# Third block of a three-block decoder: the 16 meta rows stored in zero-padded tiles of 128 rows

## The reference, cut to what matters

```
x = first_block(x, ...)            # gated linear attention, sliding window, MoBA
x = second_block(x, ...)           # mixers, dense and expert feed-forward, gated inputs
return third_block(x, meta_tokens_3, ...)

third_block:
    h = concat([meta (16 rows), x (256 rows)])         # 272 keys
    h = h + hybrid_mixer(rmsnorm(h))    # 8 heads of latent attention (MLA) and
                                        # 8 heads of sparse attention (DSA: an index picks
                                        # 64 keys for each query)
    h = h + swiglu(rmsnorm(h))
    return rmsnorm(h)[:, 16:]
```

## Time and profile before

| | us |
|---|---|
| median of 3 runs | 1898.78 |
| lowest and highest run | 1895.74, 1899.84 |
| span of the profiled execution, first to last instruction | 1895.5 |
| TensorE busy | 1844.5 (97%) |
| DVE, ACT, POOL busy | 1401.9, 1203.6, 67.4 |

### The profile page before, as it was taken

The page is one execution under the profiler, slowest core; times in us unless marked ns, Lnnn a source line. Parts: engine busy times, 40 slices in busy tenths (PEclk is TensorE's granted clock), DMA queues, the critical chain, the costliest instruction groups (busy, mean ns, idle before and its releaser), DMA issues.

```text
span 1895.5 us, 31983 instructions
## 1 busy us (share of the span) xinstructions
PE 1844.5 (97%) x11013; PEld 1598.6 (84%) x11013; DVE 1401.9 (74%) x2038; ACT 1203.6 (64%) x1897; POOL 67.4 (4%) x106
## 2 busy tenths in 40 slices
PE   8999999999999999999999999999999999999998
PEld 7969889899989888888788888888887898789997
DVE  5575765865566768998989898989899677565555
ACT  6556555544456557877777787877777665354444
POOL 2000000000000020000000000000000034000000
PEclk9989999999999989999999999999999999999999
DMA  8526334465546459999999999999999342136552
GB/s 299 192 90 220 114 134 132 143 199 188 188 156 212 147 189 367 371 371 363 365 371 371 364 372 363 360 366 359 365 361 332 123 146 89 34 100 200 184 192 91
DMA packets 129571, 454.05 MB, mean 240 GB/s; under 512 B 15182, under 2 KB 20206, under 8 KB 129216
## 3 DMA queue, kind: packets, MB, share of 16 engines
q1 hardware_dynamic: 119920, 435.74, 65.1%
q10 hardware_dynamic: 8544, 13.30, 2.2%
q0 software_dynamic: 1008, 3.67, 0.5%
HBM read 450.53 MB, written 5.27 MB: 240 GB/s over the span
## 4 chain that ended last, share of the span: by engine, by line
PE 91%; DVE 5%; ACT 3%; issue 1%; DMA 0%; ACTq 0%; DVEq 0%
PE ps L276 27%; PE ps L277 27%; PE ps L278 27%; PE ps L1069 2%; PE ps L1052 1%; DVE low L261 1%; PE ps L2737 1%; DVE xT_low L342 1%; PE ps L973 1%; PE ps L2803 1%; PE ps L1080 1%; PE ps L410 1%; ACT xT_high L330 1%; ACT high L252 1%; PE ps L309 0%
## 5 line engine op out<-in xcount | busy, mean ns | idle before, releaser
L261 DVE TENSOR_TENSOR low<-ring,high 128x1024 fp32r<-128x1024 f32 x828 | 978.9, 1221 | 213.1 <-ACT high L252 210.9
L252 ACT CAST high<-ring 128x1024 fp32r<-128x1024 f32 x828 | 833.3, 1050 | 191.6 <-PE ps L278 161.4
L276 PE MATMUL ps<-high,xT_high 128*128 128x256 f32 (+2 forms) x1848 | 639.7, 346 | 19.2 <-DVE xT_low L342 6.5
L277 PE MATMUL ps<-low,xT_high 128*128 128x256 f32 (+2 forms) x1848 | 622.7, 337 | 0.0
L278 PE MATMUL ps<-high,xT_low 128*128 128x256 f32 (+2 forms) x1848 | 619.9, 335 | 0.0
L276 PEld LDWEIGHTS ps<-high,xT_high 128*128 128x128 f32 (+1 forms) x1848 | 347.3, 188 | 61.7 <-issue 14.2
L278 PEld LDWEIGHTS ps<-high,xT_low 128*128 128x128 f32 (+1 forms) x1848 | 347.4, 188 | 40.4
L277 PEld LDWEIGHTS ps<-low,xT_high 128*128 128x128 f32 (+1 forms) x1848 | 348.2, 188 | 33.2
L276 PE MATMUL ps<-high,smallT_high 128*128 128x512 f32 (+2 forms) x582 | 225.2, 387 | 0.8 <-DVE smallT_low L342 0.5
L277 PE MATMUL ps<-low,smallT_high 128*128 128x512 f32 (+2 forms) x582 | 225.2, 387 | 0.0
L278 PE MATMUL ps<-high,smallT_low 128*128 128x512 f32 (+2 forms) x582 | 224.3, 385 | 0.0
(11 more groups left out here) (353 smaller groups left out, 1435.0 us busy)
## 6 DMA issues: line engine op xcount, KB each, us to landing
ring<-in_stream SPq DMA_DIRECT2D x828, 512.0 KB, 5.1
bias_rows<-bias_line ACTq DMA_DIRECT2D x2, 1536.0 KB, 13.5
wide<-in_wide_rows ACTq DMA_DIRECT2D x5, 512.0 KB, 5.6
work<-bias_rows ACTq DMA_DIRECT2D x2, 1024.0 KB, 9.7
h<-in_x SPq DMA_DIRECT2D x2, 512.0 KB, 4.9
work<-bias_rows ACTq DMA_DIRECT2D x2, 512.0 KB, 6.5
token_rows<-mix ACTq DMA_DIRECT2D x1, 1024.0 KB, 4.6
consts<-in_consts ACTq DMA_DIRECT2D x1, 870.0 KB
```

Of the source, the lines that this page charges most:

```text
L252: A.e.copy(k.high[:, slot, cols], k.ring[:, slot, cols]).then_inc(flow.high_made, 1)
L261: V.e.tensor_tensor(k.low[:, slot, cols], k.ring[:, slot, cols], k.high[:, slot, cols].bitcast(F32), ALU.subtract).then_inc(flow.split, 1)
L276: T.e.matmul(out, x[0], w[0], start=start, stop=False, **more)
L277: T.e.matmul(out, x[0], w[1], start=False, stop=False, **more)
```

## The change

The meta rows get tiles of full height. `probM` has 128 rows instead of 16; POOL sets it, the meta area of `proj` and the third tile of `kv` to zero, after DVE has left the experts (`experts_left`); ACT waits for `meta_cleared` before its first evacuation in the third block. The transposes of the meta rows read 128 rows and write 128 columns, of which the next transpose overwrites the last 112. The products of the meta block contract over 128 rows.

```diff
-        self.probM = buf("probM", [META, 2, NT, P])
+        self.probM = buf("probM", [P, 2, NT, P])
...
 def key_columns(dst, src):
-    return ([(src(NT)[0:META], META)] + [(src(t), P) for t in range(NT)], dst)
+    return ([(src(NT), META)] + [(src(t), P) for t in range(NT)], dst)
...
-                ins = T.e.transpose(k.ps[0:width, self.banks[n % nb], at:at + rows], src,
-                                    k.const("ident", rows)[:, 0:rows])
+                ins = T.e.transpose(k.ps[0:width, self.banks[n % nb], at:at + P], src, k.const("ident"))
                 at += rows
...
-        ins = A.e.copy(k.probM[:, h % 2, :, :].rearrange("p b w -> p (b w)"), a.meta_rows(k))
+        ins = A.e.copy(k.probM[0:META, h % 2, :, :].rearrange("p b w -> p (b w)"), a.meta_rows(k))
...
 def after_experts_dve(V, k):
     moe_add_dve(V, k, 1 if V.again else 0)
+    V.tell(V.e.memset(k.small[0:1, 222:223], 0.0), k.s["experts_left"])
     turn_first_dve(V, k, "ple1")
...
+        self.meta_rows = k.proj[:, 5120:6368]
+        self.meta_values = self.meta_rows[:, 736:1248]
...
-            lambda h, b: self.kv[0:self.blocks[b][1], tile_of[b], h * P + 64:(h + 1) * P], self.blocks,
+            lambda h, b: self.kv[:, tile_of[b], h * P + 64:(h + 1) * P], self.blocks,
...
-                return self.prm[:, 736 + h * 64:736 + (h + 1) * 64]
+                return self.meta_values[:, h * 64:(h + 1) * 64]
...
 # block3_pe, the index keys (and likewise the rotary keys, 128:160, into bank 6)
-    for rows, src in ((META, b3.prm[:, 160:224]), (P, b3.pr[:, 0, 160:224]), (P, b3.pr[:, 1, 160:224])):
-        ins = T.e.transpose(k.ps[0:64, INDEX_JOB_BANKS[0], at:at + rows], src, k.const("ident", rows)[:, 0:rows])
+    for rows, src in ((META, b3.meta_rows[:, 160:224]), (P, b3.pr[:, 0, 160:224]), (P, b3.pr[:, 1, 160:224])):
+        ins = T.e.transpose(k.ps[0:64, INDEX_JOB_BANKS[0], at:at + P], src, k.const("ident"))
...
 # block3_act
     scaled(A, k)
+    A.e.wait_ge(*A.next(k.s["meta_cleared"]))
     evac3_act(A, k, b3, 0, 0, 224)
...
 # block3_pool
+    G.e.wait_ge(k.s["experts_left"], 1)
+    G.step(G.e.memset(b3.meta_rows, 0.0))
+    G.step(G.e.memset(b3.kv[:, NT, :], 0.0))
+    G.tell(G.e.memset(k.probM[:, :, :, :], 0.0), k.s["meta_cleared"])
     G.e.wait_ge(k.s["evac"], evac + 1)
```

More of the change, by code:

```diff
@@ L129 @@
     "added all_chosen angled angles_made bias_loaded bias_made centred chosen_made cleared conv_high conv_low "
-    "conv_made conv_z copied counted diagonal diff down_high down_loaded down_made down_ready down_split ends "
+    "conv_made conv_z copied counted diagonal diff experts_left down_high down_loaded down_made down_ready down_split ends "
     "evac expd exped exps ffn_added ffn_made final_done final_loaded gained gated gated_mm gla_done gla_made "
@@ L133 @@
     "ke_made kept ki_copied ki_turned kr_copied kr_turned kv_added left line_stored logged masked masked_l "
-    "meta_parts meta_turned mixed mla_roped normed ones_set out_stored outed p_loaded params parts_high parts_low "
+    "meta_parts meta_turned mixed meta_cleared mla_roped normed ones_set out_stored outed p_loaded params parts_high parts_low "
     "plain pool_roped probs_turned prod prod_out qk_roped reduced relu_made root route_made routed router_loaded "
@@ L3143, in keys_job @@
     def keys_job(self, dst, lo, mlo, width):
-        return [(self.prm[:, mlo:mlo + width], META)] + [(self.pr[:, t, lo:lo + width], P) for t in range(NT)], dst
+        return [(self.meta_rows[:, mlo:mlo + width], META)] + [(self.pr[:, t, lo:lo + width], P) for t in range(NT)], dst
     def mla(self, k):
@@ L3375, in after5 @@
             at = 0
-            for rows, src in ((META, b3.prm[:, 128:160]), (P, b3.pr[:, 0, 128:160]), (P, b3.pr[:, 1, 128:160])):
-                ins = T.e.transpose(k.ps[0:32, 6, at:at + rows], src, k.const("ident", rows)[:, 0:rows])
+            for rows, src in ((META, b3.meta_rows[:, 128:160]), (P, b3.pr[:, 0, 128:160]), (P, b3.pr[:, 1, 128:160])):
+                ins = T.e.transpose(k.ps[0:32, 6, at:at + P], src, k.const("ident"))
                 at += rows
```

## The result

| | before | after |
|---|---|---|
| median of 5 runs each | 1898.78 | 1883.54 |
| span of the profiled execution | 1895.5 | 1880.8 |

The ratio is 0.9925, 95% interval 0.9913 to 0.9937: 14 us faster (15.2 in the medians), where 9.4 were forecast, and outside the forecast range. Two more sets of five runs of the same changed kernel gave 0.9946 (0.9933 to 0.9958) and 0.9928 (0.9916 to 0.9941). The mean of the three is 0.9933, 12.7 us. That is the gain to be explained, 3.3 us more than forecast. One of the 85 later runs of the kernel before took 3625.42 us at full clock, for a reason that isn't known; it is in no figure here.

The account below looks back on a forecast made before the run. TensorE was taken as the bound. Savings of 4.3 + 3.5 + 1.1 + 0.2 + 0.5 less 0.2 for POOL made 9.4 us, so 1898.8 became 1889.4 us; range 1886 to 1893 (0.72), 8 in 10 from 1885 to 1896.

Parts of the forecast that it names:

- The price of a change of row count: On TensorE, each change of row count between neighbouring instructions was taken to cost some 0.14 us.
- MLA products: Ten products per MLA head, 8 heads: 0.55 us saved in seven and 0.46 in the first, 4.3 us.
- the plain 0.112: Time taken for each TensorE product of 128 rows that follows one of equal row count: 0.112 us.
- DSA products: Ten products per DSA head, 8 heads: 0.41 us saved in six, 0.55 and 0.46 in the others, 3.5 us.
- Transposes: Wider meta transposes on TensorE: 1.1 us saved in MLA's keys, 0.2 in two other lines, 0.5 in DSA's keys.
- POOL: POOL's clearing of 2784 columns, 7 to 15 us, hidden under 50 us of cover; 0.2 us lost beside DVE.
- POOL in DVE's way: Rival: POOL's clearing shuts DVE out for up to 15 us, giving 1904.5 us; slower through POOL or otherwise had 0.05.
- DVE becomes the bound: Rival: DVE bounds the MLA steps, half of 4.3 us lost, 1891.5 us; clock, DVE or banks together had 0.12.
- Rows don't matter: Rival: TensorE's longer distances come from something that stays, so no change, 1899.6 us; chance 0.11.
- the clock eats part of the gain: Rival: TensorE's 1.2 GHz stretches, about 1.6 us each, shift the time, 1886 to 1893 us; clock, DVE or banks had 0.12.
- the wider range: The forecast's range for 8 in 10, from 1885 to 1896 us.

Follow-up runs that it names:

- rows64: Changed kernel with the meta block's products contracting over 64 rows instead of 128, transposes kept at 128; 1891.69 us, ratio 0.9974 to the kernel before.
- meta_together: Kernel before, 16 rows kept, with the first query tile's two products swapped so both tiles' meta products stand together; 1890.74 us, ratio 0.9967.
- last_thin: Changed kernel with the meta products of only the last two sparse heads back at 16 rows; 1888.73 us, ratio 0.9947 to the kernel before.
- last_wide: Kernel before with 128 rows only in the transposes and the last two sparse heads' meta products; 1891.65 us, ratio 0.9973.
- transposes_only: Changed kernel with the meta products back at 16 rows, the transposes kept at 128; 1893.71 us, ratio 0.9981 to the kernel before.

## Why the prediction was wrong

- **The price of a change of row count** (0.14 us): right. Reordering gave 0.16 and 0.13.
- **MLA products** (4.3 us): 0.61 us a step instead of 0.55. The first wide product starts its successor 0.06 us after itself, not 0.11, which the plain 0.112 left out. To DSA's first scores 4.98 were gained, with DSA's keys in it, against 4.8 forecast.
- **DSA products** (3.5): 0.41 us a step, as forecast.
- **Transposes** (1.1 + 0.2 + 0.5): 1.26 us for the first two against 1.3, and 0.3 for DSA's keys, where the banks let less through than I took; inside the bounds.
- **POOL** (0.2): no loss that the traces show. It cleared at about 0.9 ns a column, outside the bounds of 2.5 to 5.5 that I took from its arithmetic; with 50 us of cover it didn't matter. *POOL in DVE's way* and *DVE becomes the bound* did not come.
- **Rows don't matter** fell: `rows64` and `meta_together` put the cost on the change.
- **The clock** is the term that failed. The sum has none. I had a rival by which the clock eats part of the gain, treated stretches at 1.2 GHz as scatter of either sign, and gave them room down to 1886 us. The runs show a share with a sign, some 3 us: the change is worth 12.7 us with the waits as they are, 9.5 with them filled, and 9.7 by the steps. A part of it, 1.2 to 2.2 us, is the stretch behind the last head, which comes by way of the thin products of the last two heads (`last_thin`, `last_wide`). Where the rest lies isn't shown; at the start of the sparse attention the traces of before without a filling there have 3.4, 10.2 and 3.4 us at 1.2 GHz, those of the changed kernel 3.4, 3.4, 3.4 and none. The row for it was there: the DSA window had a granted clock of 0.93, with one stretch at its start and one at its end. I should have asked what the change does to the work just before each.
- **The median.** The first five runs lay another 2 us to the good side; more runs of the same kernel took that back. Both together put the result outside: the mean of the changed kernel's 15 runs, 1885.1, lies at the edge of the wider range (from 1885), the first median of 1883.54 beyond it.

What stays open: why products with a change of row count bring the clock down, whether by the gaps that they leave (the ten products of a last head take 1.58 us instead of 1.06 to 1.17) or by the fewer rows at work. `rows64` has the same gaps, four times the rows, and still the stretch (0.89), which speaks for the gaps, but it is one trace. At the start of the sparse attention the traces have stretches from none to 10.2 us: none in the four with wide transposes and thin MLA products (`transposes_only`, `rows64`, `last_wide` twice), 3.4 us or more in the five with thin transposes and no filling there. Why one comes or not wasn't tried beyond the filling. Padding DSA's scores to 128 rows as well, which would take away the two changes that are left in each of its steps, wasn't tried either: its copies would have to double where the banks already rule.

## What to carry to other kernels

Where small products stand between full ones on TensorE, read the distance from start to start, not the length: here equal row counts next to each other ran at 0.11 us, each change between 16 or 64 and 128 rows cost 0.13 to 0.16, and zeros up to 128 rows cost TensorE nothing. Before padding, see whether an order with fewer changes will do. And when a change makes the work before a wait denser, put the granted clock of that stretch into the sum as a term with a sign, then check it with the waits filled in both kernels.

## What the runs showed of the hardware that I had not expected

- The clock behind the last head went with the products of two heads: with eight instructions of 16 rows among the last twenty, TensorE ran at 1.2 GHz for 6.8 us behind the same wait of 0.82 us; with 128 rows it stayed at 2.4 GHz.
- Eleven idle products of 0.22 us in waits of 0.95 and 1.5 us kept TensorE at 2.4 GHz there, but the changed kernel's time gained nothing that could be told from scatter.
- Two 64-row matmuls in different halves of the rows started 0.01 us apart (`rows64`, 1655.36).
- POOL cleared 1248 columns of 128 rows in 1.14 us, 0.9 ns each, where its additions and products took 0.65 us for 256.
